# Seven-product units in the down stages of a feed-forward part, and two blocks turned later

## The reference

```
h = rms_norm(x, norm_ffn_pre[l])
f = (jax.nn.silu(h @ w_ffn_gate[l]) * (h @ w_ffn_up[l])) @ w_ffn_down[l]
x = x + rms_norm(f, norm_ffn_post[l])
```

## Time and profile before

| what | value |
|---|---|
| median of 3 runs (2287.0 to 2287.56) | 2287.12 us |
| the profiled execution's own time | 2287.35 us |
| its span, first to last instruction | 2285.4 us |
| TensorE, VectorE, ScalarE busy in the span | 2274.2, 1571.0, 1208.2 us |
| granted TensorE clock | 1.00 throughout |

### The profile page before, as it was taken

How to read it: one execution, slowest core, us unless ns; L and a number is a source line. 1 busy time by engine, 2 the same in 40 slices (tenths; PEclk the granted TensorE clock), 3 DMA queues, 4 the chain that set the end, 5 groups by cost and what they waited for, 6 DMA issues and landing times.

```text
span 2285.4 us, 27693 instructions
## 1 busy us (share of the span) xinstructions
PE 2274.2 (100%) x10681; PEld 1904.7 (83%) x10681; DVE 1571.0 (69%) x2058; ACT 1208.2 (53%) x1576; POOL 25.5 (1%) x35
## 2 busy tenths in 40 slices
PE   9999999999999999999999999999999999999998
PEld 7888888888888888888888888888888888888887
DVE  6677777756666668886677676675668755676864
ACT  6555655444445755554554454565555446556443
POOL 0000000000000000000000000000000000000000
PEclk9999999999999999999999999999999999999999
DMA  8566665766667556566666566756565665656564
GB/s 298 176 196 196 196 190 167 226 203 203 193 206 271 174 173 233 188 212 227 203 205 210 177 206 225 254 168 193 167 180 164 220 211 149 200 157 189 172 197 136
DMA packets 258578, 452.03 MB, mean 198 GB/s; under 512 B 23600, under 2 KB 63536, under 8 KB 257808
## 3 DMA queue, kind: packets, MB, share of 16 engines
q1 hardware_dynamic: 258016, 449.74, 62.2%
q10 hardware_dynamic: 432, 0.53, 0.1%
HBM read 434.99 MB, written 2.10 MB: 191 GB/s over the span
## 4 chain that ended last, share of the span: by engine, by line
PE 94%; DVE 4%; ACT 1%; issue 1%; DMA 0%; SPq 0%; DVEq 0%; ACTq 0%
PE pm L1086 28%; PE pm L1088 28%; PE pm L1087 28%; PE pb L730 1%; DVE wl L2430 1%; DVE raw L2438 1%; PE pb L912 1%; DVE wl L2444 1%; PE pb L810 1%; PE pb L1007 1%; PE pb L1009 0%; PE pb L1008 0%; PE pm L1007 0%; PE pm L1008 0%; PE pm L1009 0%
## 5 line engine op out<-in xcount | busy, mean ns | idle before, releaser
L2444 DVE TENSOR_TENSOR wl<-raw,wh 128x1024 fp32r<-128x1024 f32 (+2 forms) x746 | 897.4, 1209 | 580.1 <-ACT wh L1622 576.7
L1622 ACT ACTIVATE wh<-raw 128x1024 fp32r<-128x1024 f32 (+2 forms) x746 | 775.7, 1045 | 793.9 <-PE pm L1088 749.2
L1086 PE MATMUL pm<-wh,hTh 128*128 128x512 f32 x702 | 275.1, 392 | 0.8 <-DVE wl L2444 0.8
L1087 PE MATMUL pm<-wl,hTh 128*128 128x512 f32 x702 | 273.3, 389 | 0.0
L1088 PE MATMUL pm<-wh,hTl 128*128 128x512 f32 x702 | 273.3, 389 | 0.0
L1086 PE MATMUL pm<-wh,xT3h 128*128 128x512 f32 (+1 forms) x640 | 249.1, 389 | 0.0
L1088 PE MATMUL pm<-wh,xT3l 128*128 128x512 f32 (+1 forms) x640 | 244.6, 382 | 0.0
L1087 PE MATMUL pm<-wl,xT3h 128*128 128x512 f32 (+1 forms) x640 | 244.4, 382 | 0.0
L1087 PE MATMUL pm<-wl,x2Th 128*128 128x512 f32 x544 | 211.6, 389 | 0.0
L1086 PE MATMUL pm<-wh,x2Th 128*128 128x512 f32 x544 | 211.6, 389 | 0.0
L1088 PE MATMUL pm<-wh,x2Tl 128*128 128x512 f32 x544 | 211.6, 389 | 0.0
(11 more groups left out here) (469 smaller groups left out, 3704.8 us busy)
## 6 DMA issues: line engine op xcount, KB each, us to landing
raw<-in_w_in SPq DMA_DIRECT2D x286, 512.0 KB, 3.7
raw<-in_w_ffn_gate SPq DMA_DIRECT2D x88, 512.0 KB, 4.4
raw<-in_w_ffn_up SPq DMA_DIRECT2D x88, 512.0 KB, 5.8
raw<-in_w_ffn_down SPq DMA_DIRECT2D x88, 512.0 KB, 4.2
raw<-in_w_o SPq DMA_DIRECT2D x64, 512.0 KB, 4.3
raw<-in_w_in SPq DMA_DIRECT2D x68, 256.0 KB, 3.3
raw<-in_w_branch_b SPq DMA_DIRECT2D x32, 512.0 KB, 3.7
raw<-in_w_out SPq DMA_DIRECT2D x32, 512.0 KB, 4.6
```

The costliest lines, as they stand in the source:

```text
L1086: e.matmul(o, ah[:, kk, t], h[:, c], start=first and not begun, stop=False)
L1087: e.matmul(o, ah[:, kk, t], l[:, c], start=False, stop=False)
L1622: e.activation(h[:, 0:n], r[:, 0:n], ACT.Copy).then_inc(s["hi"], 1)
L2444: e.tensor_tensor(l[:, 0:n], r[:, 0:n], h[:, 0:n].bitcast(F32), ALU.subtract).then_inc(s["lo"], 1)
```

## The change

- `ds{q}0` and `ds{q}2` are new seven-product units ahead of `d{q}0` and `d{q}2`, for q = 0, 1, 2: the first four slices of two neighbouring down groups. The down groups keep eight steps of twelve. A down stage becomes 7 + 8 + 8 + 7 + 8 + 8 = 46 steps.
- Their operand forms are made from the first block of part q behind `fg4`, `fg7` and `fg10` (`SHAPED`), in `craw`, `crows` and a second `sform`, which lie over `X`. So SyncE saves X in device memory (`kept`, four DMAs of 512 KB, one behind the carrying of each of blocks 0 to 3), VectorE's `forms` waits for all four, and SyncE brings X back from the end of `ds22` on.
- `ds{q}0` gathers in `CD` (over `X`), `ds{q}2` in C11 to C22, two steps behind the unit. For q = 0 VectorE adds C and PSUM into `facc`. For q = 1 and 2 it adds PSUM to C in place, and GpSimd adds C to `facc` by accumulating DMAs (one of 1 MB, then four of 256 KB). fs9's first copy waits for these, 14 steps behind its start, `d30`'s addition waits for the last four.
- The second half of C's addition to `fu{c}` comes seven steps later (`PRODUCT - 2`), and b22 waits for one half less.
- Blocks 5 and 8 are turned, carried and split behind `d03` and `d13` instead of behind their `fu` (`turned`).

```diff
@@ -52,7 +52,8 @@
 SUMS = {"b11": ("t1", 0, 1, 0), "b21": ("t3", 1, 3, 1), "t1": ("t2", 0, 3, 0), "b22": ("t4", 2, 2, 0)}
-PRODUCT, SQUARED, CARRIED, SPLIT, GATHERED = 9, 11, 14, 27, 7
+SHAPED = (4, 7, 10)
+PRODUCT, SQUARED, CARRIED, SPLIT, GATHERED, LATER = 9, 11, 14, 27, 7, 14
@@ -138,7 +139,10 @@
         for c in range(4):
-            add(f"d{part}{c}", f"fT{part % 2}", rows, 512 * c, kts=range(4 * n), ev=("a", 1) if part == 0 else ("d", 2))
+            if part < 3 and c % 2 == 0:
+                seven(f"ds{part}{c}", f"fT{part % 2}", (f"d{part}{c}", f"d{part}{c + 1}"),
+                      [rows[:, 512 * i:512 * i + 512] for i in (c, c + 1)], part + 1)
+            add(f"d{part}{c}", f"fT{part % 2}", rows, 512 * c, kts=range(4 if part < 3 else 0, 4 * n), ev=("d", 2))
@@ -247,6 +252,7 @@
         self.steps = n
+        self.turned = {c: self.end[f"fu{c}"] for c in range(11)} | {5: self.end["d03"], 8: self.end["d13"]}
@@ -403,8 +409,11 @@
     m.srows = at("srows", [128, 4, T], 216)
-    m.sform = [at(f"sform{i}", [128, 4, 2, 128], 208 + 4 * i, F32R) for i in range(2)]
-    m.C11, m.C12, m.C21, m.C22 = (at(n, [128, 512], o) for n, o in (("C11", 216), ("C12", 218), ("C21", 220), ("C22", 8.5)))
+    m.sform = [[at(f"sform{n}{i}", [128, 4, 2, 128], o + 4 * i, F32R) for i in range(2)] for n, o in ((0, 208), (1, RC))]
+    m.crows = at("crows", [128, 4, T], RC + 8)
+    m.craw = at("craw", [128, 4, 2, 128], RC + 12)
+    m.CG = [at(n, [128, 512], o) for n, o in (("C11", 216), ("C12", 218), ("C21", 220), ("C22", 8.5))]
+    m.CD = at("CD", [128, 2, 2, 512], RC + 8)
@@ -618,10 +635,19 @@
         for c in range(11):
-            yield from across(m.squares[2], "d_f", p.end[f"fu{c}"] + CARRIED, [("f_t", c + 1), ("f_l", 2 * c)], m.fcross)
+            yield from across(m.squares[2], "d_f", p.turned[c] + CARRIED, [("f_t", c + 1), ("f_l", 2 * c)], m.fcross)
+            if c < 4:
+                w.wait_ge(s["xr"], 8)
+                e.dma_start(kept[:, :, part(c)], m.X[:, :, part(c)]).then_inc(s["d_kept"], 16)
...
         spread(m.BC2, a["norm_ffn_post"])
+        for c in range(4):
+            yield p.end["ds22"] + 2 + 3 * c
+            w.wait_ge(s["mm"], p.end["ds22"])
+            w.wait_ge(s["d_fa"], 96)
+            w.wait_ge(s["d_kept"], 64)
+            e.dma_start(m.X[:, :, part(c)], kept[:, :, part(c)]).then_inc(s["d_back"], 16)
@@ -694,6 +720,18 @@
     inverse_root("r0")
+    for q in (1, 2):
+        for c in (0, 2):
+            name = f"d{q}{c + 1}"
+            w.wait_ge(s["ev_d"], p.evac[name])
+            if q == 2:
+                w.wait_ge(s["d_fa"], 16 if c == 0 else 80)
+            if c == 0:
+                e.dma_start(m.facc[:, :, 0:1024], m.CD[:, :, :, :].rearrange("p h i n -> p h (i n)"), accum_op=ALU.add
+                            ).then_inc(s["d_fa"], 16)
+            else:
+                for i, C in enumerate(m.CG):
+                    e.dma_start(m.facc[:, i // 2, part(2 + i % 2)], C[:, :], accum_op=ALU.add).then_inc(s["d_fa"], 16)
@@ -975,33 +1013,35 @@
+        act, S = m.acts[g.act], m.sform[g.forms > 0]
...
+        if g.forms:
+            w.wait_ge(s["f_l"], 2 * PARTS[g.forms - 1][0] + 2)
...
-                out, lhs, b = B[:, 0, :], [[x[:, 3, k, :] for k in range(2)] for x in m.sform], None
+                out, lhs, b = B[:, 0, :], [[x[:, 3, k, :] for k in range(2)] for x in S], None
...
-                bank[b] = ("q_c", c) if b == 4 else ("q_d", 4 * c)
...
+                bank[b] = ("q_c", u) if b == 4 else ("q_d", 4 * u)
+                w.wait_ge(s["s_l"], g.forms + 1)
...
-                w.wait_ge(s[f"ev_{before.ev[0]}"], p.evac[before.name])
+                w.wait_ge(s[f"ev_{before.ev[0]}"], p.evac[before.name] - (form == "b22"))
@@ -1161,11 +1201,29 @@
-    def forms_high():
-        yield p.first["fg0"] + 6
-        w.wait_ge(s["s_d"], 5)
-        e.activation(m.sform[0][:, :, :, :], m.sraw[:, :, :, :], ACT.Copy).then_inc(s["s_h"], 1)
+    def forms_high(n, at0):
+        yield at0
+        w.wait_ge(s["s_d"], 5 * n + 5)
+        if n > 1:
+            w.wait_ge(s["mm"], p.end[f"ds{n - 2}2"])
+        e.activation(m.sform[n > 0][0][:, :, :, :], (m.craw if n else m.sraw)[:, :, :, :], ACT.Copy).then_inc(s["s_h"], 1)
+    def first_taken(name):
+        yield p.first[name] + (LATER if name == "fs9" else 2)
+        w.wait_ge(s["mm"], p.first[name] + 1)
+        if name[:2] == "ds":
+            c, q = int(name[3]), int(name[2])
+            if q == 2:
+                w.wait_ge(s["d_fa"], 16 if c == 0 else 80)
+            if c == 0:
+                w.wait_ge(s["s_l"], q + 2)
+            if c:
+                w.wait_ge(s["f_m"], 2 * (PARTS[q + 1][0] + PARTS[q + 1][1]) - 2)
+        elif name == "fs9":
+            w.wait_ge(s["d_fa"], 80)
+        e.activation(m.gather(name)[0], m.pb[4][:, :], ACT.Copy).then_inc(s["q_c"], 1)
@@ -1562,29 +1620,26 @@
                 if c:
-                    yield p.first[f"fs{c}"] + 2
-                    w.wait_ge(s["mm"], p.first[f"fs{c}"] + 1)
-                    e.activation(m.C11[:, :], m.pb[4][:, :], ACT.Copy).then_inc(s["q_c"], 1)
+                    yield from first_taken(f"fs{c}")
                 else:
-                    yield from forms_high()
+                    yield from forms_high(0, p.first["fg0"] + 6)
...
                     w.wait_ge(s["ev_d"], p.evac[f"fg{c}"])
...
+                    C = m.gather(f"fs{c}")
+                    for half, of in ((0, C[0]), (1, C[2])):
+                        e.activation(m.FST[c % 2][:, half, :], of, ACT.Silu, scale=m.rs["r0"][:, half:half + 1]
...
                     taken(0, f"fg{c}", m.FST[c % 2], ACT.Silu, "r0")
-            if q == 1:
-                for c in range(4):
-                    yield p.end[f"d0{c}"]
-                    acc = m.pm[p.acc[f"d0{c}"]]
-                    w.wait_ge(s["mm"], p.end[f"d0{c}"])
-                    w.wait_ge(s["xr"], 8)
-                    e.activation(m.facc[:, :, part(c)], acc[:, :, :], ACT.Copy).then_inc(s["ev_a"], 1)
+                if c in SHAPED:
+                    yield from forms_high(SHAPED.index(c) + 1, p.end[f"fg{c}"] + 8)
+            if q:
+                yield from first_taken(f"ds{q - 1}0")
+                yield from first_taken(f"ds{q - 1}2")
@@ -1734,48 +1789,65 @@
-    def forms():
-        yield p.first["fg0"] + 3
-        w.wait_ge(s["xt_l"], 4)
-        (h, l), R, S = m.x2T, m.srows, m.sraw
+    def forms(n, at0):
+        (h, l), R, S = (m.fT[(n - 1) % 2], m.crows, m.craw) if n else (m.x2T, m.srows, m.sraw)
+        yield at0
+        if n:
+            w.wait_ge(s["f_l"], 2 * PARTS[n - 1][0] + 2)
+            w.wait_ge(s["d_kept"], 64)
+            if n == 3:
+                w.wait_ge(s["d_fa"], 16)
+        else:
+            w.wait_ge(s["xt_l"], 4)
...
         e.tensor_tensor(R[:, :, :], h[:, 0:4, :].bitcast(F32), l[:, 0:4, :].bitcast(F32), ALU.add).then_inc(s["s_d"], 1)
...
-        yield p.first["fg0"] + 7
-        w.wait_ge(s["s_h"], 1)
-        e.tensor_tensor(m.sform[1][:, :, :, :], S[:, :, :, :], m.sform[0][:, :, :, :].bitcast(F32), ALU.subtract
-                        ).then_inc(s["s_l"], 1)
-    def gathered(c):
-        n = 4 * c - 4
-        yield p.end[f"fs{c}"] + GATHERED
-        w.wait_ge(s["mm"], p.first[f"fs{c}"] + 6)
-        if c > 1:
-            w.wait_ge(s["f_m"], 2 * c - 2)
-        w.wait_ge(s["q_c"], c)
-        w.wait_ge(s["f_s"], 2 * c - 2)
...
-    def joined(name, halves, value):
-        yield p.end[name]
+        yield at0 + 4
+        w.wait_ge(s["s_h"], n + 1)
+        hi, lo = m.sform[n > 0]
+        e.tensor_tensor(lo[:, :, :, :], S[:, :, :, :], hi[:, :, :, :].bitcast(F32), ALU.subtract).then_inc(s["s_l"], 1)
+    def gathered(name):
+        u, (C11, C12, C21, C22) = p.unit[name], m.gather(name)
+        yield p.end[name] + (2 if name[0] == "d" else GATHERED + 4 if name == "fs9" else GATHERED)
+        w.wait_ge(s["mm"], p.first[name] + 6)
+        w.wait_ge(s["q_c"], u + 1)
+        if name[0] == "f":
+            c = int(name[2:])
+            w.wait_ge(s["f_s"], 2 * c - 2)
+            if c > 1:
+                w.wait_ge(s["f_m"], 2 * c - 2)
+        e.tensor_tensor(C12, C11, m.pb[6][:, :], ALU.add).then_inc(s["q_d"], 1)
...
+    def joined(unit, i, half, into=None):
+        name, C = p.g[unit].joins[i], m.gather(unit)[2 * half + i]
         w.wait_ge(s["mm"], p.end[name])
-        w.wait_ge(s["q_d"], value)
-        for half, C in enumerate(halves):
-            e.tensor_tensor(C[:, :], C[:, :], banks(name)[:, half, :], ALU.add).then_inc(s["ev_d"], 1)
+        w.wait_ge(s["q_d"], 4 * p.unit[unit] + 4)
+        e.tensor_tensor(C if into is None else into, C, banks(name)[:, half, :], ALU.add).then_inc(s["ev_d"], 1)
+    def down(q):
+        for c in (0, 2):
+            unit = f"ds{q}{c}"
+            yield from gathered(unit)
+            for i in range(2):
+                yield p.end[f"d{q}{c + i}"]
+                for half in range(2):
```

(109 more changed lines are left out.)

41 lines of the change are left out of this document (18 added, 23 removed).

## The result

The changed kernel took **2299.53 us** (median of 5, 2295.79 to 2300.14) where the kernel before, run beside it, took 2287.47 (2287.0 to 2287.88). The ratio is 1.0047, its 95% interval 1.0036 to 1.0058: slower by 12 us, more than the 0.2% (4.6 us) that the prediction took as the grain, and outside the forecast range of 2279.5 to 2290.5. The five executions of the kernel after fall in two groups, three at 2299.5 to 2300.1 and two at 2295.8, so a difference taken from its median is good to some 4 us only, and the places of the losses are read from the profiled execution.

What follows compares the result with a forecast made beforehand. TensorE was taken as the bound, busy for the whole span. Matmuls -8.16, old losses -3.0 and new losses +10.5 gave -0.7 us from 2287.35, so 2286.7, or 2286.5 as median; range 2279.5 to 2290.5.

Steps and rivals of the forecast that it cites:

- the steps that go: In the down stages, units do in 7 steps what took 8; 6 steps of 1.36 us go, -8.16 us.
- the moved half: Half of a block's last C addition, 0.6 us, leaves the unit's window; late units 2 to 6 and 8 become quiet.
- the save of X: Behind fg4, VectorE's forms wait 6.2 us for the fourth save, landing taken as 3.9; fs5 loses 6.7, plus 0.1.
- Rival A: The save lands before VectorE reaches the forms behind fg4; fs5 loses 1.0 only, 2280.6 us; chance 0.32.
- 1.0 each in fs8 and ds20: The forms' low part puts 1.14 us into the unit's window and 0.6 leaves; fs8 and ds20 lose 1.0 us each.
- the turned blocks: Blocks 5 and 8 turned behind the down stage: their fT pair falls into fs7 and fs10, quiet, nothing late.
- the step on the accumulating DMAs: GpSimd's accumulating DMAs for parts 1 and 2 fit the room before their readers: zero loss, upper end 2 us.
- Rival C: Saves, reloads and accumulates delay reloading behind a unit: 1 to 2 us in three places, 2289 to 2292; chance 0.13.
- Rival B: GpSimd's DMA issues hold VectorE, 1.04 us at each of six issues, 6.2 us on top: 2292.7; chance 0.10.

Runs made afterwards that it cites:

- the experiment on the kernel before: The kernel before with only the second half of C's addition to fu moved seven steps later and b22 waiting for one half less: 2285.31 us, ratio 0.9988.
- the last experiment: Kernel after with saves a block earlier, VectorE adding instead of accumulating DMAs, forms earlier, CD's additions and X's return later: 2279.07 us, ratio 0.9963.

## Why the prediction was wrong

**Right: the steps that go.** TensorE kept its pitch in the new units; -8.16 us stands.

**Right: the moved half.** The prediction put 1.1 us of quiet units in place of 3.0 us of old losses. The distances of the units and the experiment on the kernel before (-2.6) agree.

**Right: the save of X.** The landing was taken as 3.9 and was 3.75 (issued at 1001.08, forms at 1004.83); VectorE stood 6.3 where 6.2 was forecast, and 6.9 us went lost where it was 6.8. By the Trainium skill (DMA: Bandwidth & Descriptors, Anatomy of one DMA) the prediction also gave 3.2 us for the landing; that section's fit is for DMAs issued by GpSimd, SyncE issued this one, and the row was nearer. Rival A, the save in time, did not come, and its price of 5.8 was what moving the save gave back (5.9 in the list of losses, 6.8 between the medians).

**Right: 1.0 each in fs8 and ds20**, and the turned blocks did no harm.

**Wrong: "Covered even at 14.2: zero, upper end 2"**, the step on the accumulating DMAs. Its bounds of 3 and 14.2 us held for 1 MB in one DMA (9.5 and 11.5); for the same bytes in four DMAs they did not (15.2 and 19.5 us from the first issue to the last landing). The step compared each landing with the room until its own reader, and left out two things. First, what the transfer does to its neighbours: it takes the DMA engines for twice the time of a copy of its bytes, and the loads of `raw` that should refill six buffers behind ds12, in block 9 and behind ds22 came late. ScalarE then stood 5.0 and 5.8 us behind ds12 and ds22, past the 4.1 (a wait of 1.64 and 2.5 of slack) that the prediction itself had read from the earlier trace rows. In block 9 it stood 3.1, which reached nobody by itself, but the carrying of the block came late too (3.0) and with it fs10. That is 1.1, 2.0 and 3.7 us more than forecast; 1.6 of the 3.7 are the slow matmuls described below. With plain copies in the same places nothing is lost behind ds12 and at fs10. Second, the room at d30, 10.9 less 1.5 us and 5.7 on top, 15.1 in all, was held against one landing of 14.2 at most; four in sequence, with a pause after the first and with weights and memory tokens loaded beside them, took 19.5 us, 4.4 more than the room. VectorE stood 10.6 us and TensorE 4.65: 6.7 us with the slow matmuls behind it.

**Rival C** named this mechanism and put it at "1 to 2 us in three places", 2289 to 2292, with a chance of 0.13. It was the right case and far too cheap; the time came out 13 us above the forecast. Its price was read from the bytes ("at 1 MB more in that stretch, 2.5 us"), and an accumulating MB cost as much engine time as two. It also had no term for the wait at d30, the largest of the four. The range ended inside that price, at 2290.5.

**Rival B**, GpSimd's issues holding VectorE, was not seen. In VectorE's timeline of the kernel after, two splits beside three issues take 2.50 us, as the pair of the earlier trace rows did:

```profile
1318.05 2.50 DVE L2508 TENSOR_TENSOR wl<-raw,wh 128x1024 fp32r<-128x1024 f32 x2
```

## What to carry to other kernels

Price a new DMA twice: by its own landing against its reader, and by the engine time that it takes from the loads beside it, stretch by stretch. A share of the DMA engines near 1 is no loss by itself (the last experiment had 1.04); what counts is whether the loads behind the new transfer still land within the slack of their reader. An addition by DMA cost twice a copy here, and four VectorE operations of 0.6 us a unit, in steps where TensorE was not waiting for VectorE, did the same for next to nothing (the last experiment). Several small steps that together decide one wait must be put in a row with their queue, not each compared with the room alone.
